# Root mean squares ahead of feed-forward blocks and gates: one fp32 product and ScalarE's logarithm and exponential in place of column sums, a GpSimd power and turns

## What is computed

```python
def rmsnorm_2(x, gain):
    y = xf * lax.rsqrt(jnp.mean(xf * xf, axis=-1, keepdims=True) + EPS)
    return (y * gain.astype(jnp.float32)).astype(x.dtype)

for layer in range(DEPTH_2):                      # 4
    h = x + 0.5 * swiglu(rmsnorm_2(x, g[0]), w_ffn_gu[layer, 0], w_ffn_down[layer, 0])
    mix = mixer(rmsnorm_2(h, g[1]))
    h = h + mix
    h = h + 0.5 * swiglu(rmsnorm_2(h, g[2]), w_ffn_gu[layer, 1], w_ffn_down[layer, 1])
    gate = jax.nn.sigmoid(rmsnorm_2(h, g[3]) @ w_ple_gate[layer])
    x = h + gate * (p[layer] @ w_ple_proj[layer])
```

## Time and profile before

| | |
|---|---|
| runs | 2412.53, 2413.33, 2420.59 us; median 2413.33 |
| the profiled execution | 2411.01 us |
| its span, first to last instruction | 2408.8 us |
| TensorE busy (matmuls) | 2396.9 us |
| VectorE busy | 1725.2 us |
| ScalarE busy | 1317.2 us |
| GpSimd busy | 90.1 us |
| weights and inputs read | 414.62 MB, 173 GB/s over the span |

### The profile page before, as it was taken

One profiled execution on the slowest core, in us unless ns is written; L12 is line 12 of the kernel. 1 busy time (PEld: TensorE's weight loads), 2 busy tenths in 40 slices (PEclk: granted clock), 3 DMA queues, 4 the chain that ended last, 5 costly groups with the idle time before them and its releaser, 6 DMA issues.

```text
span 2408.8 us, 51817 instructions
## 1 busy us (share of the span) xinstructions
PE 2396.9 (100%) x20462; PEld 2367.8 (98%) x20462; DVE 1725.2 (72%) x2425; ACT 1317.2 (55%) x2019; POOL 90.1 (4%) x91
## 2 busy tenths in 40 slices
PE   9999999999999999999999999999999999999999
PEld 9999999999999999999999999999999999999999
DVE  8878867668776686667766776688667766877666
ACT  5756655447654464454644554466445544765444
POOL 1000000001100000000000000000000000220000
PEclk9999999999999999999999999999999999999999
DMA  7315327565365546545465566644665655535663
GB/s 270 116 63 173 123 79 227 190 195 164 120 196 194 190 158 221 194 164 194 146 204 191 178 199 195 196 133 136 198 195 180 201 192 192 164 126 185 197 195 124
DMA packets 115378, 418.86 MB, mean 174 GB/s; under 512 B 12832, under 2 KB 14112, under 8 KB 114976
## 3 DMA queue, kind: packets, MB, share of 16 engines
q1 hardware_dynamic: 114096, 412.40, 52.3%
q0 software_dynamic: 560, 2.10, 0.3%
q10 hardware_dynamic: 576, 2.27, 0.3%
HBM read 414.62 MB, written 2.10 MB: 173 GB/s over the span
## 4 chain that ended last, share of the span: by engine, by line
PE 94%; DVE 3%; ACT 2%; DMA 1%; issue 0%; ACTq 0%; SPq 0%; DVEq 0%
PE ps_gu L140 17%; PE ps_gu L146 17%; PE ps_gu L141 17%; PE ps_acc L140 8%; PE ps_acc L146 8%; PE ps_acc L141 8%; PE ps_acc L2740 1%; PE ps_acc L2298 1%; DVE w_lo L100 1%; PE ps_misc L140 1%; PE ps_gu L2334 1%; PE ps_misc L146 1%; PE ps_misc L141 1%; PE ps_sum L140 1%; PE ps_sum L146 1%; PE ps_sum L141 1%
## 5 line engine op out<-in xcount | busy, mean ns | idle before, releaser
L100 DVE TENSOR_TENSOR w_lo<-w_raw,w_hi 128x1024 fp32r<-128x1024 f32 x781 | 953.0, 1228 | 373.8 <-ACT w_hi L92 366.3
L140 PE MATMUL ps_gu<-xn_hi,w_hi 128*128 128x256 f32 x3832 | 1053.3, 279 | 1.7 <-DVE w_lo L100 0.8
L141 PE MATMUL ps_gu<-xn_hi,w_lo 128*128 128x256 f32 x3832 | 1044.9, 276 | 0.0
L92 ACT ACTIVATE w_hi<-w_raw 128x1024 fp32r<-128x1024 f32 x781 | 819.3, 1056 | 355.0 <-PE ps_gu L146 260.4
L146 PE MATMUL ps_gu<-xn_lo,w_hi 128*128 128x256 f32 x3832 | 1009.1, 276 | 0.0
L140 PEld LDWEIGHTS ps_gu<-xn_hi,w_hi 128*128 128x128 f32 x3832 | 719.3, 188 | 4.7 <-issue 2.3
L141 PEld LDWEIGHTS ps_gu<-xn_hi,w_lo 128*128 128x128 f32 x3832 | 719.4, 188 | 0.3
L146 PEld LDWEIGHTS ps_gu<-xn_lo,w_hi 128*128 128x128 f32 x3832 | 696.7, 188 | 0.0
L140 PE MATMUL ps_acc<-h_hi,w_hi 128*128 128x256 f32 x1496 | 414.4, 277 | 0.0
L146 PE MATMUL ps_acc<-h_lo,w_hi 128*128 128x256 f32 x1496 | 413.2, 276 | 0.0
L141 PE MATMUL ps_acc<-h_hi,w_lo 128*128 128x256 f32 x1496 | 413.2, 276 | 0.0
(11 more groups left out here) (472 smaller groups left out, 2638.4 us busy)
## 6 DMA issues: line engine op xcount, KB each, us to landing
w_raw<-in_w_dram SPq DMA_DIRECT2D x781, 512.0 KB, 4.0
const<-in_const_dram SPq DMA_DIRECT2D x1, 1216.0 KB, 8.5
distance_rows<-arena POOLq DMA_DIRECT2D x1, 1024.0 KB, 7.6
p_all<-distance_rows POOLq DMA_DIRECT2D x2, 512.0 KB, 5.5
p_all<-in_p_dram ACTq DMA_DIRECT2D x1, 1024.0 KB, 6.4
out_dram<-x_res SPq DMA_DIRECT2D x8, 128.0 KB, 1.9
x_res<-in_x_dram ACTq DMA_DIRECT2D x1, 512.0 KB, 6.7
x_res<-in_x_dram SPq DMA_DIRECT2D x1, 512.0 KB, 6.1
```

The costliest lines, as they stand in the source:

```text
L92: act.activation(self.w_hi[:, s, :], self.w_raw[:, r, :], ACT.Copy).then_inc(self.w_hi_ready.sem, 1)
L100: dve.tensor_tensor(self.w_lo[:, s, :], self.w_raw[:, c % NR, :], self.w_hi[:, s, :], ALU.subtract)\
L140: pe.matmul(out, self.w_hi[:, s, j0:j0 + width], rhs_hi, start=start, stop=False, skip_group_check=True)
L141: pe.matmul(out, self.w_lo[:, s, j0:j0 + width], rhs_hi, start=False, stop=False, skip_group_check=True)
```

## The change

- `fold_step` folds all eight tiles to one: its last step adds tile 7 to 6, then 1 to 0, then 6 to 0 (three adds where one was). So the nine norms with three tiles left now have one.
- Ahead of feed-forward blocks and gates, `sum_rows` takes the place of `sum_squares`: one fp32 product of a constant 128 x 128 tile `means`, filled with 1/1024, with the folded tile (256 columns). It puts the mean of each token in every partition, as rows. `root_rows` on ScalarE then takes the logarithm of mean plus epsilon and the exponential of -0.5 times that, into `rstd`. No GpSimd step, no transposes, no copy. The tables of logarithm and exponential are loaded ahead, and that of silu or sigmoid behind the roots; in `ffn` the high half of chunk g+6 goes ahead of the roots.
- With the inner norm, both means are summed behind the fifth group of tile 1 and no longer in `first`; VectorE makes the argument of the outer root from both (`outer`), behind the low halves of tile 0, and ScalarE takes two logarithms and two exponentials (`roots`).
- Norms ahead of hybrid layers and mixers keep columns, power and transposes, with the one folded tile.

```diff
-def fold_six(k, dve, n, a, squares, folded):
+
+
+def fold_step(k, dve, n, a, squares, folded):
     step = k("square_step")
     if n == 0:
         dve.wait_ge(*squares)
@@ -249,8 +247,12 @@
         dve.wait_ge(*step.made())
         dve.tensor_tensor(a[:, 0:2, :], a[:, 0:2, :], a[:, 4:6, :], ALU.add).then_inc(*step.up())
     else:
+        dve.wait_ge(*squares)
+        dve.tensor_tensor(a[:, 6, :], a[:, 6, :], a[:, 7, :], ALU.add)
         dve.wait_ge(*step.made())
-        dve.tensor_tensor(a[:, 0, :], a[:, 0, :], a[:, 1, :], ALU.add).then_inc(*k(folded).up())
+        dve.tensor_tensor(a[:, 0, :], a[:, 0, :], a[:, 1, :], ALU.add).then_inc(*step.up())
+        dve.wait_ge(*step.made())
+        dve.tensor_tensor(a[:, 0, :], a[:, 0, :], a[:, 6, :], ALU.add).then_inc(*k(folded).up())
...
     def sum(self, pe):
         k = self.k
         pe.wait_ge(*k("inner_folded").at(1))
-        pe.wait_ge(*k("inner_square_made").at(KD))
-        for m in (0, 6, 7):
-            for tt in range(TT):
-                mm = pe.matmul(k.ps_sum[:, TT + tt:TT + tt + 1], self.squares[:, m, tt * P:(tt + 1) * P], k.ones[:, 0:1],
-                               start=False, stop=(m == 7), skip_group_check=True)
-        return mm
-
-    def root(self, pool):
+        return pe.matmul(k.ps_sum[:, S:2 * S], k.means[:, :], self.squares[:, 0, :], start=False, stop=True,
+                         skip_group_check=True)
...
+    def outer(self, dve):
         k, step = self.k, self.k("inner_step")
-        pool.tensor_tensor(k.outer_col[:, :], k.mean_sq[:, :], k.eps[:, :], ALU.mult).then_inc(*step.up())
-        pool.wait_ge(*step.made())
-        pool.tensor_tensor(k.outer_col[:, :], k.outer_col[:, :], k.inner_sq[:, :], ALU.add).then_inc(*step.up())
-        pool.wait_ge(*step.made())
-        return pool.tensor_tensor(k.rcol[:, :], k.outer_col[:, :], k.powers[:, 0:TT], ALU.pow)
-
-    def inner_root(self, pool):
-        k = self.k
-        pool.tensor_tensor(k.inner_col[:, :], k.mean_sq[:, :], k.powers[:, 0:TT], ALU.pow).then_inc(*k("inner_step").up())
-
-    def turned(self, pe):
-
-
-        k = self.k
-        pe.wait_ge(*k("inner_step").at(3))
-        pe.wait_ge(*k("rstd_ready").at(k.norms))
-        for tt in range(TT):
-            mm = pe.transpose(k.ps_sum[:, tt * P:(tt + 1) * P], k.inner_col[:, tt:tt + 1].to_broadcast([P, P]), k.ident)
-        mm.then_inc(*k("inner_rows").up())
+        dve.wait_ge(*k("mean_rows").at(k.row_norms))
+        dve.tensor_scalar(k.rstd[:, :], k.ps_sum[:, 0:S], EPS, EPS * EPS, ALU.mult, ALU.add).then_inc(*step.up())
+        dve.wait_ge(*step.made())
+        dve.tensor_tensor(k.rstd[:, :], k.rstd[:, :], k.ps_sum[:, S:2 * S], ALU.add).then_inc(*k("outer_ready").up())
+
+    def roots(self, act):
+
+
+        k, step = self.k, self.k("inner_root")
+        act.wait_ge(*k("outer_ready").at(1))
+        act.activation(k.rstd[:, :], k.rstd[:, :], ACT.Ln).then_inc(*step.up())
+        act.activation(self.rows, k.ps_sum[:, 0:S], ACT.Ln, bias=k.eps[:, 0:1]).then_inc(*step.up())
+        act.wait_ge(*step.made(1))
+        act.activation(k.rstd[:, :], k.rstd[:, :], ACT.Exp, scale=-0.5).then_inc(k("rstd_ready").sem, 1)
+        act.wait_ge(*step.made())
+        act.activation(self.rows, self.rows, ACT.Exp, scale=-0.5).then_inc(*k("inner_ready").up())
...
+def sum_rows(k, pe, n):
+
+
+    k.row_norms += 1
     pe.wait_ge(*k("misc_free").made())
-    tiles, squares = k.summed if summed is None else summed
     pe.wait_ge(*k("squares_folded").at(n))
-    pe.wait_ge(*squares)
-    for m in tiles:
-        for tt in range(TT):
-            mm = pe.matmul(k.ps_sum[:, tt:tt + 1], k.xn[:, m, tt * P:(tt + 1) * P], k.ones[:, 0:1],
-                           start=(m == 0 and tt == 0), stop=(m == tiles[-1]), skip_group_check=True)
+    if k.row_norms == 1:
+        pe.wait_ge(*k("means_ready").made())
+    mm = pe.matmul(k.ps_sum[:, 0:S], k.means[:, :], k.xn[:, 0, :], start=True, stop=True, skip_group_check=True)
     if k.inner:
         mm = k.inner.sum(pe)
+    mm.then_inc(*k("mean_rows").up())
+
+
+def root_rows(k, act):
+
+
+    if k.inner:
+        return k.inner.roots(act)
+    act.wait_ge(*k("mean_rows").at(k.row_norms))
+    act.activation(k.rstd[:, :], k.ps_sum[:, 0:S], ACT.Ln, bias=k.eps[:, 0:1]).then_inc(*k("root_step").up())
+    act.wait_ge(*k("root_step").made())
+    act.activation(k.rstd[:, :], k.rstd[:, :], ACT.Exp, scale=-0.5).then_inc(k("rstd_ready").sem, 1)
...
@@ -483,7 +482,8 @@
             high(KD - 1)
             low(KD - 2)
             low(KD - 1)
-            sum_squares(k, pe)
+            if not k.inner:
+                sum_rows(k, pe, k.norms)
         def tile(t, i):
             if t == 0:
@@ -498,10 +498,8 @@
                     mm = k.products(pe, k.ps_gu[t % 2][:, n * S:(n + 1) * S], c % NS, j * P, P,
                                     k.xn_hi[:, j, :], k.xn_lo[:, j, :], False, j == KD - 1,
                                     start=(n == 0 and j == 0))
-                    if t == 1 and n == 0 and j == (6 if k.inner else 4):
-                        rstd_rows(k, pe)
-                    if t == 1 and n == 1 and j == 2 and k.inner:
-                        k.inner.turned(pe)
+                    if t == 1 and n == 0 and j == 4 and k.inner:
+                        sum_rows(k, pe, k.norms)
...
+            behind = t == 0 and late[1]
             if t == 0:
-                act.preload_act_table(ACT.Silu)
-                root_in(k, act)
-            behind = t == 0 and late[1]
+                act.preload_act_table_set("natural_log_exp_and_others")
             if not behind:
                 k.hi(act, g + 1 + AHEAD, i)
+            if t == 0:
+                root_rows(k, act)
+                act.preload_act_table(ACT.Silu)
...
-                take_rstd(k, dve)
+                if k.inner:
+                    k.inner.outer(dve)
                 dve.wait_ge(*k("rstd_ready").at(k.norms))
...
-        sum_squares(k, pe, n, summed)
+        sum_rows(k, pe, n)
...
-                if m == 2 and j == 0:
-                    rstd_rows(k, pe, n)
-                if m == 2 and j == 4:
-                    pe.wait_ge(*k("rstd_ready").at(n))
-                    for tt in range(TT):
-                        pe.transpose(k.ps_sum[:, S + tt * P:S + (tt + 1) * P], k.rcol[:, tt:tt + 1].to_broadcast([P, P]),
-                                     k.ident)
             mm.then_inc(k.chunk_done.sem, 1)
     @block.scalar
     def _(act):
-        act.preload_act_table(ACT.Sigmoid)
+        act.preload_act_table_set("natural_log_exp_and_others")
         for j in range(3):
             k.hi(act, c0 + j + AHEAD)
-        root_in(k, act, n)
+        root_rows(k, act)
+        act.preload_act_table(ACT.Sigmoid)
...
-        take_rstd(k, dve, n)
...
+        pool.memset(k.means[:, :], 1.0 / D).then_inc(*k("means_ready").up())
```

More of the change, by code:

```diff
@@ L194, in __init__ @@
         self.squares = k("square_made").n
-        self.tiles = (0,) if squares < KD else (0, 6, 7)
         k.norms += 1
@@ L372, in sum_squares @@
     if k.inner:
         mm = k.inner.sum(pe)
-    mm.then_inc(k("sum_sq_col").sem, 1)
-def root_in(k, act, n=None):
-    n = n or k.norms
-    act.wait_ge(*k("sum_sq_col").at(n))
-    if k.inner:
-        act.activation(k.inner_sq[:, :], k.ps_sum[:, TT:2 * TT], ACT.Copy, scale=1.0 / D)
+    mm.then_inc(*k("mean_rows").up())
[6 more added lines that the diff above has]
+    act.activation(k.rstd[:, :], k.rstd[:, :], ACT.Exp, scale=-0.5).then_inc(k("rstd_ready").sem, 1)
@@ L383, in root_in, with sum_squares @@
+def sum_squares(k, pe):
+    pe.wait_ge(*k("misc_free").made())
+    pe.wait_ge(*k("squares_folded").at(k.norms))
+    for tt in range(TT):
+        mm = pe.matmul(k.ps_sum[:, tt:tt + 1], k.xn[:, 0, tt * P:(tt + 1) * P], k.ones[:, 0:1],
+                       start=(tt == 0), stop=True, skip_group_check=True)
+    mm.then_inc(k("sum_sq_col").sem, 1)
+def root_in(k, act):
+    act.wait_ge(*k("sum_sq_col").at(k.column_norms))
     act.activation(k.mean_sq[:, :], k.ps_sum[:, 0:TT], ACT.Identity, scale=1.0 / D, bias=k.eps[:, 0:1])\
@@ L411, in rstd_rows, with take_rstd @@
     mm.then_inc(k("rstd_rows").sem, 1)
-def take_rstd(k, dve, n=None):
-    n = n or k.norms
-    dve.wait_ge(*k("rstd_rows").at(n))
+def take_rstd(k, dve):
+    dve.wait_ge(*k("rstd_rows").at(k.column_norms))
     dve.tensor_copy(k.rstd[:, :], k.ps_sum[:, 0:S]).then_inc(k("rstd_ready").sem, 1)
@@ L640, in ple @@
     proj = lambda m: k.ps_acc[:, m // 2, (m % 2) * S:(m % 2 + 1) * S]
-    n, summed = k.norms, k.summed
+    n = k.norms
     nxt = None if next_gain is None else Norm(k, next_gain)
@@ L774, in setup @@
     k.eps = k.sb("eps", [P, TT])
-    k.inner_sq, k.inner_col, k.outer_col = (k.sb(n, [P, TT]) for n in ("inner_square_columns", "inner_columns", "outer_columns"))
     k.both_gains = k.sb("both_gains", [P, KD])
     k.inner = None
-    k.norms = 0
+    k.norms = k.row_norms = k.column_norms = 0
```

(1 more changed line is left out.)

32 lines of the change are left out of this document (9 added, 23 removed).

## The result

| | before | after |
|---|---|---|
| median | 2412.93 us (2411.59 to 2420.59) | 2463.39 us (2461.63 to 2471.78) |
| ratio | | 1.0209, 95% interval 1.0178 to 1.0241 |
| profiled execution | 2411.01 us | 2461.63 us |
| its span | 2408.8 us | 2459.6 us |

The forecast was 2404.9 us. The change costs some 50 us where 8 were to be won, and 2463 lies far outside the range.

What follows compares the result with a forecast made beforehand. TensorE's matmuls were taken as the bound (2396.9 of 2408.8 us). Terms -4.5 - 2.2 - 1.8 - 0.9 + 0.95 = -8.4 us gave 2402.6 profiled, 2404.9 median; forecast 2403 to 2407 (0.70), range 2400.4 to 2410.5.

Steps and rivals of the forecast that it cites:

- A pace 0.006 us slower per product: TensorE between the sum and the next wait: may vanish or stay, 0.1 us a norm, counted as nothing.
- The product with the means: Added on TensorE at each changed norm: one fp32 product of 256 columns, 0.45 us, bounds 0.43 and 0.55.
- Rival 5: At the norms, the product with means takes four passes instead of two: 5.6 us of gain lost, 2410.5 us; chance 0.03.
- Second first_layer: Column norm of the second first_layer: six sums become two, 0.9 us saved.
- Gates: At the four gates: sums and turns replaced by one product, nothing newly waits, 0.45 us saved each, 1.8 in all.
- Mixer FFNs: Four FFNs behind a mixer: no wait, first hidden tile ready 0.9 us early, 4 x 1.12 = 4.5 us gained.
- Behind a gate: Three FFNs behind a gate: new TensorE wait of 0.4 us for a low half, so 0.72 us gained each, 2.2 together.
- Inner norm: FFN with the inner norm: longer VectorE and ScalarE chain makes TensorE wait 3.3 us; 0.95 us lost instead of 2.25 won.
- rival 4: On ScalarE, logarithm and exponential each get their own table load: +18.3 us, time 2423 us; chance 0.05.
- rival 3: On ScalarE, a hidden drain of about 1.38 us at each table switch: +3.4 us, 2408.3 us; chance 0.05.
- Rival 2: At the inner norm, TensorE's clock falls in the wait: 1.9 us lost, 2406.8 us; chance 0.07.

Runs made afterwards that it cites:

- turns_back: The changed kernel with two transposes nobody reads put back behind the fifth group of tile 1 in seven FFNs: 2447.00 us.
- turns_at_once: The changed kernel with two transposes nobody reads directly behind the product with the means in seven FFNs: 2428.19 us.
- halves_one_pass: The changed kernel, first chunk of tile 1 as 16 high then 8 low products in all FFNs, outer ahead of two low halves, one-pass fp32r sum: 2409.60 us.
- halves: The changed kernel with the first chunk of tile 1 done as 16 high products, then 8 low ones, in seven FFNs: 2408.11 us.
- fold_halves: The kernel before with only the fold to one tile, plus 16 high then 8 low products in tile 1's first chunk, turns between, seven FFNs: 2466.14 us.
- one_pass: The changed kernel with means and folded squares in fp32r, so that the sum is one pass: 2429.58 us.
- late_sum: The kernel before with two column products (four fp32 records, no reader) added behind the seventh group of tile 1 in seven FFNs: 2475.35 us.
- halves_turns: The changed kernel with tile 1's first chunk as 16 high, two idle turns, then 8 low products in seven FFNs: 2471.93 us.
- halves_next: The changed kernel with the second chunk of tile 1 done as 16 high, then 8 low products in seven FFNs: 2407.87 us.
- outer_first: The changed kernel with VectorE's outer ahead of the two low halves of tile 0 in the first FFN: 2462.47 us.
- all_halves: The changed kernel, tile 1's first chunk as 16 high then 8 low products in all eight FFNs, outer ahead of two low halves: 2404.14 us.

## Why the prediction was wrong

**The step that failed** is the last one of the sum: "A pace 0.006 us slower per product, seen between the sum and the next wait, may vanish or stay: 0.1 us a norm, counted as nothing." The size per product was right (0.0056). The number of products was not. I gave "stay" only the stretch where the trace of before showed it, 15 products, when staying means all 1584 of the FFN. The earlier trace rows held what was needed to ask: the slow stretch ends at an instruction, L410, that the change takes away. An unknown that persists should have been costed at both ends: 0.1 us a norm, or 8.9 an FFN. With seven of them the rival on the slower side is 2404.9 + 62 = 2467 us; mine had been extra table loads. My first reading after the result, that the turns end the slow pace, fell too (`turns_back`): they only set it anew.

**The other steps held.**
- The product with the means: 2244.87 - 2244.32 - 0.12 = 0.43 us (taken as 0.45), two records. Rival 5 is out.
- Second first_layer: the sums and the product behind them went from 1.46 to 0.57 us, 0.89 won (0.9).
- Gates: 2.32 us from the sum to the change, as before, and no turns: 0.46 won (0.45).
- Mixer FFNs: no wait. From the sum to `down` 6.14 us, where 5.9 was said; the 48 products' slow pace makes 0.27 of it. The first tile was ready 1.06 us ahead (0.9 said).
- Behind a gate: the timeline of TensorE has the wait, 0.34 us (0.4 said), three times:

```profile
910.27 0.35 PE L140 MATMUL ps_gu<-xn_hi,w_hi 128*128 128x256 f32 x1 [0.34 <-DVE w_lo L100]
```

- Inner norm: 3.05 us for `h_lo` (3.3 said). VectorE's low halves began at 369.09, not 370.1, and `outer` at 372.50, not 373.6; TensorE's 48 products also ended 0.9 us earlier than said, so the wait came out nearly right. Both have one cause: the prediction added its delays to times of the old trace and left out what its own sum had already saved upstream. In after the first product of the inner FFN's tile 1 starts at 368.14, where the sums began at 369.27 before, and everything behind it starts about 1 us earlier.
- ScalarE's chain in after, at the FFN of the earlier trace rows:

```profile
2245.43 0.46 ACT L374 ACTIVATE rstd<-ps_sum,eps 128x256 f32<-128x256 f32 x1
2245.92 0.42 ACT L376 ACTIVATE rstd<-rstd 128x256 f32<-128x256 f32 x1
2246.36 1.28 ACT L523 ACT_TABLE_LOAD   x1
2247.65 0.38 ACT L527 ACTIVATE silu<-ps_gu 128x256 f32<-128x256 f32 x1
```

No load stands between logarithm and exponential, which rules out rival 4. The silu begins 0.01 us behind the end of its load, which rules out rival 3. The Trainium skill ("ScalarE: Activation LUTs", What ACT_TABLE_LOAD costs) adds a drain of 1.38 us; here, with a true function behind the load, the trace again has none.

**Rival 2, given 0.07, came true.** Timeline of TensorE in after, and windows over it with the granted clock:

```profile
374.58 0.28 PE L146 MATMUL ps_gu<-xn_lo,w_hi 128*128 128x256 f32 x1
377.91 0.48 PE L140 MATMUL ps_acc<-h_hi,w_hi 128*128 128x256 f32 x1 [3.05 <-DVE h_lo L565]
378.19 0.41 PE L141 MATMUL ps_acc<-h_hi,w_lo 128*128 128x256 f32 x1
...
381.39 0.32 PE L141 MATMUL ps_acc<-h_hi,w_lo 128*128 128x256 f32 x1
```

```profile
360.00:374.50 14.50, 14.09 (x116) 1.00 0.80 271
...
378.60:381.30 2.70, 2.70 (x15) 0.50 0.22 42
381.60:390.00 8.40, 8.40 (x76) 1.00 0.78 259
```

Behind 3.05 us of standing still the granted clock is 0.50 of full, which is 1.2 GHz, and 15 steps take 0.213 us each. From 377.91 to 381.39 it lost 3.48 - 16 x 0.1133 = 1.7 us (1.9 had been worked out). I had argued against it that no row showed a fall; but before had no idle stretch of that length in which one could have shown. The granted clock of 1.00 at the start was a poor witness: the 0.22 us of a record there is close to the 0.213 us at 0.50 here. The loss isn't tied to 3 us either. Behind 3.33 us, in `turns_at_once`, 5.3 us of window read 0.50, and behind 2.08 us, in `halves_one_pass`, the clock fell only after TensorE had been at work again for 0.8 us.

**The sum, made again**: -8.4, + 1.7 for the clock, - 0.25 for the shorter wait is -6.95. `halves`, the same change at the fast pace, has a span of 2401.7: -7.1 against before. With 58.4 us of slow steps, -6.95 gives +51.5; after measured +50.8. All known terms together miss by under 1 us.

## What to carry to other kernels

Count how many products start in a window, at the granted clock, before and after: two values with one clock show a change of pace that no view of waits shows. Where a stream of matmuls has a pace of its own behind an odd instruction, ask what ends it, and cost it for the whole stream if the change removes, adds or moves an instruction there. Here, a run of 16 high products behind the last fp32 instruction costs nothing and brings 55 us back (`halves`); behind two column sums such a run stayed slow (`fold_halves`), so it has to be tried at each place.

## What the runs showed of the hardware

- TensorE runs products of 128x256 at 0.1133 or at 0.1189 us from start to start at a granted clock of 1.00, and holds either for 1500 products and more.
- The pace is set anew by fp32 matmuls and turns. In `one_pass` and `turns_at_once` slow FFNs also stand behind a wait (0.60 and 0.12 us), and in `one_pass` the slow pace came at four of four gates with neither (137 products in 16 us, 143 in after). Four added records (`late_sum`) or two turns (`halves_turns`) made it slow in 7 of 7 FFNs. A run of high products behind the product with the means made it fast in 7 of 7 (`halves`, `halves_next`). Elsewhere the executions of one kernel differ as if it were drawn each time: a slow FFN more or less, 8.9 us, is about the step between them, before's own 2411 and 2420 us among them. No kernel has traces of two executions, so this is a reading of the times and not shown.
- Behind a wait of TensorE of 3.05 us the granted clock was 0.50 for some 3.4 us (products 0.213 us apart), and so it was behind one of 2.08 us (`halves_one_pass`). Behind 1.72 us (`outer_first`) and 1.96 us (`all_halves`) it stayed at 1.00.
- A product in one pass (fp32r) at the norm holds TensorE 0.31 us less than the fp32 one (0.240 against 0.547 us to the second product behind). In `halves_one_pass` against `all_halves` the median is no better, since waits, clock and slow stretches took it back.
